# Layer 1's gate and up projections by seven block products instead of eight, with output and head weights loaded early

## The reference

```python
def mla_mixer(...):
    def queries(a):
        q = (rmsnorm(a @ w_dq, q_lat_g) @ w_uq).reshape(b, n, MLA_HEADS, MLA_QK)
    ...
    out_l = o_l.reshape(b, n, MLA_HEADS * MLA_V) @ w_out

def swiglu(a, wg, wu, wd):
    return (jax.nn.silu(a @ wg) * (a @ wu)) @ wd

h = h + g1[:, None] * m_lat
f_lat = modulate(rmsnorm(h, norm_ffn_g[layer]), sh2[:, None], sc2[:, None])
h = h + g2[:, None] * swiglu(f_lat, ffn_w_gate[layer], ffn_w_up[layer], ffn_w_down[layer])
```

## Time and profile before

| | |
|---|---|
| median of 3 runs | 3422.99 us |
| the profiled execution's own time | 3424.26 us |
| span of the profiled execution, first to last instruction | 3422.5 us |
| PE busy | 3170.0 us, 93% |
| weight loads of PE (PEld) busy | 2603.7 us, 76% |
| DVE, ACT, POOL busy | 1838.5, 972.2, 1518.1 us |
| DMA | 297.26 MB, mean 87 GB/s |
| mean granted TensorE clock | 0.965 |

### The profile page before, as it was taken

The page is one execution under the profiler, slowest core; times in us unless marked ns, Lnnn a source line. Parts: engine busy times, 40 slices in busy tenths (PEclk is TensorE's granted clock), DMA queues, the critical chain, the costliest instruction groups (busy, mean ns, idle before and its releaser), DMA issues. The chain is left out here.

```text
span 3422.5 us, 42949 instructions
## 1 busy us (share of the span) xinstructions
PE 3170.0 (93%) x15030; PEld 2603.7 (76%) x15030; DVE 1838.5 (54%) x2468; ACT 972.2 (28%) x1698; POOL 1518.1 (44%) x1166
## 2 busy tenths in 40 slices
PE   7997987799999999999888879999997999999999
PEld 6775775588888888888677657777775788888887
DVE  5584876555444444444527747777757433333333
ACT  4322664131000000000324546666661300000000
POOL 3683444443333222332522247777787533332332
PEclk9998998899999999999989979999998999999999
DMA  6466221522222222222214872322315111111111
GB/s 225 132 187 183 55 54 38 175 63 68 62 61 68 67 67 62 61 61 66 83 40 158 261 193 57 77 65 67 75 29 157 59 50 49 49 44 41 55 49 62
DMA packets 160192, 297.26 MB, mean 87 GB/s; under 512 B 53344, under 2 KB 98144, under 8 KB 159968
## 3 DMA queue, kind: packets, MB, share of 16 engines
q1 hardware_dynamic: 148576, 254.08, 25.3%
q10 hardware_dynamic: 11520, 41.95, 4.2%
HBM read 233.06 MB, written 62.91 MB: 86 GB/s over the span
## 5 line engine op out<-in xcount | busy, mean ns | idle before, releaser
L127 POOL TENSOR_TENSOR small<-ident 128x1 f32<-128x1 f32 x170 | 53.9, 317 | 1166.7 <-PE ps L163 665.8
L163 PE MATMUL ps<-hidden,whi 128*128 128x512 f32 (+1 forms) x1760 | 501.0, 370 | 8.6 <-POOL wlo L138 5.1
L2016 DVE SCALAR_TENSOR_TENSOR residual<-ps,mod,residual 128x512 f32<-128x512 f32 (+1 forms) x440 | 302.8, 696 | 376.6 <-PE ps L163 376.6
L1340 POOL TENSOR_TENSOR a_pl<-a_p,a_ph 128x512 fp32r<-128x512 f32 x320 | 430.5, 1368 | 136.3 <-ACT a_p L1314 136.2
L138 POOL TENSOR_TENSOR wlo<-raw,whi 128x1024 fp32r<-128x1024 f32 x170 | 440.8, 2593 | 14.2
L163 PE MATMUL ps<-mixed_hi,whi 128*128 128x512 f32 (+1 forms) x1200 | 427.0, 356 | 14.6 <-POOL wlo L138 10.7
L163 PE MATMUL ps<-mixed_lo,whi 128*128 128x512 f32 (+1 forms) x1200 | 425.9, 355 | 0.0
L163 PE MATMUL ps<-mixed_hi,wlo 128*128 128x512 f32 (+1 forms) x1200 | 425.5, 355 | 0.0
L163 PEld LDWEIGHTS ps<-hidden,whi 128*128 128x128 f32 x1760 | 320.3, 189 | 65.5 <-POOL wlo L138 5.2
L1827 ACT ACTIVATE hidden<-gated 128x512 fp32r<-128x512 f32 (+1 forms) x110 | 64.9, 590 | 1000.1 <-DVE gated L2005 1000.0
L2005 DVE TENSOR_TENSOR gated<-gated,ps 128x512 f32<-128x512 f32 (+1 forms) x110 | 69.9, 635 | 511.5 <-PE ps L163 495.2
(11 more groups left out here) (292 smaller groups left out, 6093.7 us busy)
## 6 DMA issues: line engine op xcount, KB each, us to landing
raw<-in_w_ffn SPq DMA_DIRECT2D x132, 512.0 KB, 3.6
l_vraw<-in_mod_t ACTq DMA_DIRECT2D x56, 512.0 KB, 3.7
raw<-in_w_out SPq DMA_DIRECT2D x32, 512.0 KB, 3.8
a_k<-scratch_k SPq DMA_DIRECT2D x32, 480.0 KB, 6.4
f_vraw<-in_mod_t ACTq DMA_DIRECT2D x24, 512.0 KB, 4.2
a_q<-scratch_q SPq DMA_DIRECT2D x32, 384.0 KB, 5.0
a_k<-scratch_k SPq DMA_DIRECT2D x32, 320.0 KB, 7.3
a_v<-scratch_v SPq DMA_DIRECT2D x32, 320.0 KB, 5.1
```

What stands on the lines that cost most here:

```text
L127: e.nc.gpsimd.tensor_tensor(e.spare[:, 0:1], e.ident[:, 0:1], e.ident[:, 0:1], ALU.mult)
L163: last = nc.tensor.matmul(out, a, b, start=at == 0, stop=at == n - 1)
L1340: nc.gpsimd.tensor_tensor(pl[:, kk % 2, c], p[:, kk % 2, c], ph[:, kk % 2, c].bitcast(F32), ALU.subtract).then_inc(s["pl"], 1)
L2016: last = nc.vector.scalar_tensor_tensor(h[:, m, a:a + w], e.ps[:, o:o + w], e.mod[:, g, c:c + 1], h[:, m, a:a + w], ALU.mult, ALU.add)
```

## The change

Five things are changed, all around layer 1.

**Seven products.** For ten of the eleven pairs in layer 1 (layer 0 keeps its code) the gate of two hidden tiles over two token chunks is one 2x2 block product: the weight's blocks are (feature half, hidden tile), the activation's blocks (feature half, token chunk), and each block product is 4 feature blocks x 3 = 12 matmuls. Instead of 8 such products PE runs 7 (Winograd's form of Strassen's algorithm), each into its own PSUM bank (`product`), for the gate and for the up projection. An iteration has 84 + 96 + 84 matmuls. The sums it needs:

- of weights, per pair of tiles: 4 sums of 128x512 by POOL (`combine`), and 7 halves of 128x512 to split (`half`) instead of 4; w_down's blocks are split by halves too (`downs`). `whi` and `wlo` become a ring of 6 half slots. An iteration's order on POOL is `pair` (gate), `downs`, `pair` (up).
- of activations, once: ACT writes the unrounded value of all 16 units (`y`), DVE forms sums (`factors`), ACT, DVE and POOL split them (`factor_high`, `factor_low`, `third_low`).
- of products, per iteration: 7 additions for the gate and 7 for the up projection by DVE (`add_product`), one operand in SBUF and one in PSUM; ACT copies the first product out of PSUM (`first_part`). The up result now lies in SBUF when DVE multiplies it with the gate (`gated_product`).

**Loads.** The blocks of `w_ffn` of layer 1 lie in the order gate, gate, down, down, up, up, and SP waits for POOL's count of split halves.

**w_out early.** Slots of the rings are allocated before `attention1`; the first three `w_out` blocks are loaded at the end of attention's SP program and split at the end of its POOL program.

**Head weights early.** The first `w_uq` and the first `w_ukv` block are loaded at the end of layer 0's `mixer_ffn`, into memory that the heads stage then uses.

**Memory.** `dynamic_dma_scratch_size` is set to 4096, and several buffers are placed by address.

```diff
+                def free(i, old, pos):
+                    if pos < 6:
+                        if old is None:
+                            block_used(e, pool, first, 0, 1 + pos // 2)
+                        else:
+                            pool.wait_ge(s["product"], old * PRODUCTS + pos + 9)
+                    elif pos < 13:
+                        pool.wait_ge(s["product"], i * PRODUCTS + pos - 5)
+                    elif pos < 17:
+                        pool.wait_ge(s["down"], i * NB + NB + 1)
+                    else:
+                        pool.wait_ge(s["product"], i * PRODUCTS + 8)
...
+                def half(i, old, pos, of):
+                    free(i, old, pos)
+                    settle(pos)
+                    nc.gpsimd.tensor_scalar(wh[:, slot(pos), :], of, 1.0, 1.0, ALU.mult, ALU.mult).then_inc(s["half_hi"], 1)
+                    pool.wait_ge(s["half_hi"], i * HALVES + pos + 1)
+                    nc.gpsimd.tensor_tensor(wl[:, slot(pos), :], of, wh[:, slot(pos), :].bitcast(F32), ALU.subtract).then_inc(s["half"], 1)
...
+                def pair(i, old, j, p0, x0, between=None):
+                    a11, a12, a21, a22 = weight_half(j, 0), weight_half(j, 1), weight_half(j + 1, 0), weight_half(j + 1, 1)
+                    arrived(i, j)
+                    settle(HALVES + j)
+                    half(i, old, p0, a11)
+                    half(i, old, p0 + 1, a12)
+                    arrived(i, j + 1)
+                    settle(HALVES + j + 1)
+                    combine(i, x0, spare[:, :], a11, a21, ALU.subtract)
+                    combine(i, x0 + 1, a21, a21, a22, ALU.add)
+                    pool.wait_ge(s["half"], i * HALVES + p0 + 1)
+                    combine(i, x0 + 2, a11, a21, a11, ALU.subtract)
+                    half(i, old, p0 + 2, a11)
+                    half(i, old, p0 + 3, spare[:, :])
+                    if between:
+                        between()
+                    half(i, old, p0 + 4, a21)
+                    half(i, old, p0 + 5, a22)
+                    pool.wait_ge(s["half"], i * HALVES + p0 + 4)
+                    combine(i, x0 + 3, spare[:, :], a12, a11, ALU.subtract)
+                    half(i, old, p0 + 6, spare[:, :])
...
+                def load_pair(i, j, old, wait, p=mid):
+                    sl, at = p.slots[j], i * 6 + 4 + j
+                    source = w_ffn[bass.ds(at, 1), :, :].rearrange("o p f -> p (o f)")
+                    if wait:
+                        sp.wait_ge(s["half"], old * HALVES + (11, U0_ + 7, U0_ + 6, 7, 6, 9)[j])
+                    sp.dma_start(e.raw[:, sl, :], source).then_inc(e.raw_full[sl], 16)
...
+                def down_halves(i, p0):
+                    pe.wait_ge(s["half"], i * HALVES + p0 + 4)
+                    pe.wait_ge(s["lo"], i * 4 + 4)
...
+                    with each(pe, mid.iters) as i:
+                        gate_products(i)
+                        down_halves(i, D0)
+                        up_products(i)
+                    down_halves(mid.iters, 0)
...
+                    dve.wait_ge(s["first"], i * 2 + 2)
+                    add(1, 8, p2, p0)
+                    gated_product(0, p2)
+                    add(2, 9, p0, p0)
+                    add(3, 10, p1, p0)
+                    dve.wait_ge(s["uprod"], i * 4 + 5)
+                    add(4, 11, p2, p1)
+                    add(5, 11, p0, p0)
+                    gated_product(1, p2)
+                    lower(0)
...
+                    gated_product(2, p1)
+                    lower(1)
+                    add(7, 13, p0, p0)
+                    gated_product(3, p0)
+                    lower(2)
+                    lower(3)
```

More of the change, by code:

```diff
@@ L83 @@
 RING = 3
+AHEAD, NQ1 = 8, HEADS1 * QK1
 class Env:
@@ L1148, in _ @@
                     load(i * 2 + 3, 1, False)
+                sp.wait_ge(s["st"], 2 * KS * HEADS1)
+                for N in range(RING):
+                    load_block(e, sp, mixp, 0, N, w_out[N, :, :])
                 sp.wait_ge(s["x"], 16 * KT)
@@ L1353, in _ @@
                 walk(pool, step)
+                for N in range(RING):
+                    split_block(e, pool, mixp, 0, N, 1024)
 def krb_sq(krt, sq):
@@ L1497, in conditions @@
                           .then_inc(s["cond"], 16)
-                for N in range(2 * KT):
+                if ahead:
+                    conditions(cond1)
+                for N in range(ahead, 2 * KT):
                     load_block(e, sp, mixp, 0, N, w_out[N % KT, :, :])
@@ new lines, in _ @@
+                if latents:
+                    with each(pool, mid.iters) as i:
+                        for j in range(6):
+                            split_block(e, pool, mid, i, j, 1024)
+                    for j in range(2):
+                        split_block(e, pool, end, 0, j, 1024)
+                else:
+                    pool.wait_ge(s["nwhole"], UNITS)
+                    pool.wait_ge(s["lo0"], UNITS // 2)
+                    pair(0, None, 0, G0, 0, third_low)
+                    downs(0, None, 2, D0)
+                    pair(0, None, 4, U0_, 4)
+                    with each(pool, mid.iters - 1) as i:
+                        pair(i + 1, i, 0, G0, 0)
+                        downs(i + 1, i, 2, D0)
+                        pair(i + 1, i, 4, U0_, 4)
+                    n_ = mid.iters
+                    for z in range(2):
+                        pool.wait_ge(e.raw_full[end.slots[z]], end.filled(0, z))
+                        settle(HALVES + z)
+                        for c in range(2):
+                            half(n_, n_ - 1, 2 * z + c, weight_half(z, c, end))
@@ L1678, in _, with product @@
                 column(first, 0, 3, 1, 3 * BANK, s["up"], s["prod"])
+                def product(i, pos, idx, P):
+                    pe.wait_ge(s["half"], i * HALVES + pos + 1)
+                    bank = pbank[idx]
+                    first_, c_ = {1: (0, 0), 2: (4, 0), 3: (4, 1), 5: (0, 1)}.get(P, (None, None))
+                    for k in range(4):
+                        if first_ is not None:
+                            mh, ml = (v[:, first_ + k, c_ * BANK:(c_ + 1) * BANK] for v in (hi, lo))
+                        else:
+                            mh, ml = (factor[:, k, x, :] for x in {4: (1, 2), 6: (0, 3), 7: (5, 4)}[P])
+                        w = slice(k * 128, (k + 1) * 128)
+                        for x, (a, b) in enumerate(((wh, mh), (wh, ml), (wl, mh))):
+                            last = nc.tensor.matmul(e.ps[:, bank:bank + BANK], a[:, slot(pos), w], b, start=k == 0 and x == 0,
+                                                    stop=k == 3 and x == 2)
+                    last.then_inc(s["product"], 1)
@@ L1835, in _ @@
                     row(5)
-                tile(first, 0, 2, 1, 1, (6,))
-                if latents:
-                    row(7)
+                else:
+                    for k in range(4):
+                        act.wait_ge(s["tsum"], 4 * k + 4)
+                        factor_high(factor[:, k, 5, :], whole[:, k, 4, :], "thi")
+                        factor_high(factor[:, k, 0, :], whole[:, k, 3, :], "thi")
+                tile(first, 0, 2, 1, 1, (6,))
+                if not latents:
+                    block_used(e, act, first, 0, 3)
+                    for k in range(4):
+                        factor_high(hi[:, k, BANK:2 * BANK], whole[:, k, 1, :], "t1hi")
+                    for k in range(4):
+                        act.wait_ge(s["t1lo"], k + 1)
+                        factor_high(factor[:, k, 1, :], whole[:, k, 2, :], "t4hi")
+                    with each(act, mid.iters) as i:
+                        gate_pair(i)
+                        up_pair(i)
+                    return
+                row(7)
                 with each(act, mid.iters) as i:
```

282 lines of the change are left out of this document (236 added, 46 removed).

## The result

The changed kernel takes 3450.66 us (median of 4 runs, 3448.21 to 3454.85), the kernel before 3421.48 (4 runs; the three known ahead of the prediction gave 3422.99): ratio 1.009, 95% interval 1.0076 to 1.0105. It is 29 us slower. The forecast was 3442 with a range of 3404 to 3464, so direction and range were right; a change of +19 was forecast where +29 was measured, and the time was 8.7 us short. The profiled execution took 3454.85 us, 30.6 more than that of before.

A forecast was written before the change was run, and what follows sets the result against it. PE bounds the kernel before; in the changed loop POOL's serial work between down projections would. Loop +28.5, mixing's front -6, heads -4.5, norm +1 give +19 us on 3424.26, less 1.3 for the runs' median: 3442, range 3404 to 3464.

The forecast's parts named there:

- Front: Stages ahead of layer 1's feed-forward loop: early loads gain 6 us around mixing and 4.5 in heads, norm costs 1.
- the norm's +1: Norm stage: ACT writes 16 unrounded values instead of 8, costing 1 us net, bounds 0 and 4.
- POOL's price: Loop: POOL needs 2.10 us per weight half (settling, copy, subtraction) and 1.35 per sum of weights.
- undisturbed stretch: POOL's work between two down projections without DVE's disturbance: 41.7 us, including 0.7 for wake-up, branch and waits.
- Collisions: Loop: DVE's eight instructions with two SBUF operands delay POOL 0.43 us each, 3.4 us per iteration, bounds 0 and 5.4.
- The lock: Loop: DVE instructions with two SBUF inputs and POOL's SBUF reads exclude each other wholly; at full cost 18 us more.
- Clock: Down projections: PE's wait of about 4.6 us before each lowers its clock, adding 1.8 us each time.
- An iteration: Loop: down projection 21.9, clock loss 1.8 and stretch 45.1 us make 68.8 against 65.95 before.
- The first piece: From the first pair's products to the first down projection: POOL needs 21.2 us for seven halves and one sum.
- The last piece: Loop's end: a down projection of 23.7 us, then 50.6 for the last up part, down projection and addition.
- late loads: Loop: POOL waits 0.7 us per iteration for weight blocks; with full lock as alternative 3448 to 3460 us, chance 0.16.
- The PE-bound case: Loop: PE stays the bound, fewer matmuls save 55 us, total 3358 us; chance 0.05.

The follow-up runs named there:

- front_only: Kernel before the change with only the early loads of w_out's first three blocks and the two head blocks: 3410.35 us, ratio to before 0.9975.
- psum_pairs: Changed kernel, DVE's eight two-SBUF instructions per iteration reading their second operand from PSUM bank 7 (wrong values): 3419.88 us, ratio to before 1.0001.
- filler: Changed kernel with 16 extra thrown-away matmuls on PE before each down projection waits for its weight halves: 3430.92 us, ratio to before 1.0036.
- early_mid: Changed kernel with the loop's first three weight blocks loaded one by one, as soon as each raw slot is split: 3450.86 us, ratio to before 1.0093.
- act_down4: Changed kernel with only the four rounding copies of the down projection's halves moved from POOL to ACT: 3426.23 us, ratio to before 1.0014.
- act_all: Changed kernel with all 18 rounding copies of an iteration moved from POOL to ACT: 3377.47 us, ratio to before 0.987.

## Why the prediction was right, and where it was short

On the profiled executions, in the order of its steps:

- *Front.* T, the end of the first pair's products on PE, is 2725.18 - 1.18 = 2724.0 in the changed kernel, from this row:

```profile
2725.18 0.49 PE L1854 MATMUL ps<-o_hi,whi 128*128 128x512 f32 x1 [1.18 <-ACT gated L2042]
```

  Before it was 2733.8: 9.8 us earlier, forecast -6 - 4.5 + 1 = -9.5, and front_only's 9.5 by the times of the runs is near the 10.5 that the forecast has without the norm's +1. That the sum came out so well is in part luck, for its parts missed and made up for each other: attention begins 6.3 earlier (1986.84 and 1993.11; forecast 4.5). Attention itself then took 2.9 us longer in this execution. The stage from its end to the norm's last subtraction gained 6.3 (9.75 at its end, less 3.4 at its start; forecast 5). Attention's 2.9 is chance at least in part: ACT's last `a_ph` begins anywhere from 2552.0 to 2561.1 in the profiles of the other kernels with the same front (2558.5 here).
- *POOL's price.* A half was priced at 2.10 and takes 2.11. The undisturbed stretch was put at 41.7 and is 42.5, the term of 0.7 for wake-up and waits being too small (by the stretch it was 1.5, the upper bound given): in the timeline of POOL the loop's branch alone is 0.41, and the successor of a sum waits 0.16 each time. Collisions: 3.4 forecast, 3.2 measured.
- *The lock.* The Trainium skill's rule (SBUF — State Buffer, "Who interferes with whom") was weighed against 0.43 us an instruction. psum_pairs agrees with the rule in both kinds, two SBUF inputs disturb POOL and one does not, but POOL loses 0.4 on average, not the 0.69 that the instruction takes; the measurement decides. Taken as a price for each, the rule would have overstated the cost by 2.4 us an iteration.
- *Clock.* 23.7 forecast for a down projection, 23.9 measured; filler shows that the pause ahead of it is the cause. Not foreseen: a second pause of 2.1 us inside the gate's products, nine times. It lies where PE is not on the path.
- *An iteration.* 68.8 forecast, 69.53 measured: stretch +0.5, down projection +0.2. Nine times: +6.6.
- *The first piece, the step that failed.* From T to the first down projection the prediction had 21.2 us, for seven halves and one sum behind T. Measured: 2752.13 - 2724.0 = 28.1. It took POOL to be at position 4 when the first pair's products end. But POOL could not start before its block had come, at 2708.09 after 3.96 us of waiting, and four subtractions of factors, 6.41 us, which the prediction nowhere counted, stand between positions 3 and 4: position 4 began at 2731.76, 7.8 behind T; from there to the down projection it took 20.4, near the 21.2 priced. +6.9. That the four subtractions cost so much is read off the trace; no run takes them away, and early_mid, which takes the 3.96 us of waiting away, brought the down projection only 1.7 forward.
- *The last piece.* From the start of the tenth down projection to the end of the last addition 72.8, forecast 23.7 + 50.6 = 74.3: -1.5.

Together +6.9 + 6.6 - 1.5 = +12.0 in the loop and -0.3 in front of it: 11.7, and 19 + 11.7 = 30.7, the 30.6 seen. So the mechanism held, and the prices in the steady state to 0.8 us a stretch; a piece of POOL's work that occurs once was left out, and a small term was too small nine times.

Of the rivals, late loads were none in the changed kernel (POOL waits for no block in the nine iterations) and appeared as soon as POOL was relieved, in act_down4. The PE-bound case came about only in act_all, where the work that excluded it had gone.

## What to carry to other kernels

Before matmuls are traded for additions, sum what the helper engine must do between the two points where its buffers come free, in series, and compare that with PE's time in the same stretch; a share of busy time (POOL 53% here) says nothing of it. When it loses, move the cheapest instruction of its chain to an engine that idles: the 18 roundings on ACT turned a loss of 29 us into a gain of 44, and of 52 with the start mended. And count a pause of PE with what the lower clock takes afterwards, and the pieces ahead of the loop with the same care as the loop.

## What the hardware showed that was not expected

- The clock after a pause: after PE waited 1.59 us ahead of a down projection (act_down4) its window is 22.09 us long at a granted clock of 1.00, after 2.99 us it is 23.66 at 0.93, and yet after 2.97 us it is 22.10 at 1.00. The other runs have both too: after 2.32 us (filler, the first down projection) 23.51 at 0.93, after 2.93 us (psum_pairs, the last) 22.11 at 1.00. So these runs do not show what decides between the two. Behind the changed kernel's 5.0 us or 3.4 us they took 23.2 to 24.8.
- Work that is thrown away can pay: 176 more matmuls made the program 20 us faster.
- A pair of SBUF operands on DVE costs POOL 0.4 us on average (psum_pairs), and even POOL's smallest instruction pays it: a 128x1 settling operation took 0.64 to 0.70 us instead of 0.19.
